# A hybrid decoder step on one core: cached pages copied later, unused products while x is loading, and gate blocks laid between products of 16 columns

## What is computed

```
u = rmsnorm(x)
z = u @ w_in + b_in                       # 1024 x 6968: mLSTM, queries, keys/values, gates
h_m = mlstm(conv(z[mx]), z[mv], z[mo], z[mi], z[mf], state_C, state_n, state_m)
h_n = nsa(z[nq], z[nkv], z[ng], cache_kv[page_table], cache_win_kv, w_cmp)
      # three branches: compressed blocks, selected blocks, a window
g   = sigmoid(z[bg])                      # 2 x 1024 merge gates
x   = x + (g_m * (h_m @ w_bm) + g_n * (h_n @ w_bn)) @ w_out
x   = x + moe(rmsnorm(x))                 # 32 experts, top 4
y   = rmsnorm(x)
```

## Time and profile before

| | us |
|---|---|
| median of 3 runs | 1617.41 (1616.68 to 1617.52) |
| profiled execution, its own time | 1614.81 |
| its span, first to last instruction | 1613.2 |
| TensorE busy | 1512.4 (94%) |
| VectorE / ScalarE / GpSimd busy | 545.6 / 317.4 / 53.1 |

### The profile page before, as it was taken

How to read it: one execution, slowest core, us unless ns; L and a number is a source line. 1 busy time by engine, 2 the same in 40 slices (tenths; PEclk the granted TensorE clock), 3 DMA queues, 4 the chain that set the end, 5 groups by cost and what they waited for, 6 DMA issues and landing times.

```text
span 1613.2 us, 22042 instructions
## 1 busy us (share of the span) xinstructions
PE 1512.4 (94%) x8565; PEld 710.6 (44%) x8565; DVE 545.6 (34%) x1184; ACT 317.4 (20%) x711; POOL 53.1 (3%) x121
## 2 busy tenths in 40 slices
PE   8999998999888899999999999999999999999996
PEld 5447555666755565433333333333333333333332
DVE  4511333444345422442323232232322222322323
ACT  2301221244235500311111111111111111111112
POOL 5410000000000000000000000000000000000000
PEclk9999999899999999999999999999999999999999
DMA  9932456152454299399999999999999999999995
GB/s 340 392 119 105 122 179 131 54 182 103 144 157 135 85 231 393 128 380 426 428 427 427 427 428 429 427 427 427 428 429 427 427 428 427 429 427 427 427 427 223
DMA packets 99712, 507.33 MB, mean 314 GB/s; under 512 B 19126, under 2 KB 57386, under 8 KB 73896
## 3 DMA queue, kind: packets, MB, share of 16 engines
q1 hardware_dynamic: 95522, 482.78, 75.4%
q0 software_dynamic: 4080, 23.73, 3.9%
q10 hardware_dynamic: 54, 0.05, 0.0%
HBM read 499.38 MB, written 28.06 MB: 327 GB/s over the span
## 4 chain that ended last, share of the span: by engine, by line
PE 31%; DMA 30%; DVE 3%; issue 1%; SPq 0%; ACT 0%; DVEq 0%
DMA wring<-w_gu 25%; PE bank L2116 14%; PE bank L2157 8%; DMA zf<-w_gu 4%; PE bank L1968 3%; PE bank L1977 2%; PE bank L2058 1%; PE bank L1953 1%; DMA wring<-w_branch_n 1%; DVE zf L2487 1%; DVE zf L2485 1%; DVE zf L2489 1%; PE bank L1986 0%; PE bank L1949 0%; PE bank L2091 0%
## 5 line engine op out<-in xcount | busy, mean ns | idle before, releaser
L2116 PE MATMUL bank<-wring,zf 128*64 128x512 f32 x1600 | 360.5, 596 | 25.2 <-DMA wring<-w_gu 24.8
L2116 PEld LDWEIGHTS bank<-wring,zf 128*64 128x64 f32 x1600 | 108.8, 136 | 250.5 <-issue 192.4
L2469 DVE SCALAR_TENSOR_TENSOR x<-bank,wt,x 128x512 f32<-128x512 f32 x155 | 104.9, 744 | 196.5 <-PE bank L2058 196.5
L2157 PE MATMUL bank<-wring,zf 128*64 128x512 f32 x768 | 170.1, 595 | 0.7
L2200 ACT ACTIVATE zf<-bank 128x512 f32<-128x512 f32 (+1 forms) x133 | 75.8, 594 | 314.5 <-PE bank L2157 214.8
L2116 PE MATMUL bank<-zf 128*64 128x512 f32 x448 | 100.8, 596 | 6.3 <-DMA zf<-w_gu 6.3
L2475 DVE TENSOR_TENSOR zf<-bank,zf 128x512 f32<-128x512 f32 x32 | 22.1, 692 | 224.6 <-ACT zf L2200 224.6
L2157 PEld LDWEIGHTS bank<-wring,zf 128*64 128x64 f32 x768 | 53.4, 137 | 98.9 <-issue 96.9
L954 PE MATMUL bank<-uT,w_slots 128*128 128x320 f32 x256 | 80.7, 463 | 1.2 <-ACT zf L1087 1.2
L1968 PE MATMUL bank<-zf,wring 128*128 128x320 f32 x256 | 69.4, 433 | 1.7 <-PEq L1279 0.9
L2058 PE MATMUL bank<-zf,eqw 64*128 64x512 bf16 x558 | 69.3, 380 | 0.0
(11 more groups left out here) (528 smaller groups left out, 1689.3 us busy)
## 6 DMA issues: line engine op xcount, KB each, us to landing
wring<-w_gu SPq DMA_DIRECT2D x100, 2048.0 KB, 32.6
wring<-w_dn SPq DMA_DIRECT2D x48, 2048.0 KB, 34.5
zf<-w_gu SPq DMA_DIRECT2D x28, 2048.0 KB, 32.8
zf<-w_dn SPq DMA_DIRECT2D x16, 2048.0 KB, 34.4
w_slots<-w_in SPq DMA_DIRECT2D x11, 2048.0 KB, 8.8
kv_linear<-cache_kv POOLq DMA_DIRECT2D x64, 256.0 KB, 5.2
kv_stage<-kv_linear SPq DMA_DIRECT2D x16, 1024.0 KB, 9.2
w_slots<-w_in SPq DMA_DIRECT2D x4, 1024.0 KB, 8.2
```

Source lines behind the costliest of these rows:

```text
L2116: last = pe.matmul(half(2 + gu, h), xe[:, k % 4, k // 4, :], m.ring[slot(k // 2)][:, o:o + H], start=False, stop=(k == KD - 1))
L2157: last = pe.matmul(half(4, h), atT[:, k % 4, k // 4, :], m.ring[slot(4 + k // 4)][:, o:o + H], start=(k == 0), stop=(k == 7))
L2469: dve.scalar_tensor_tensor(part(r), m.bank[SCATTER_BANKS[r]][:, :], wt[:, r // 2, bass.ds(i - 1, 1)], part(r), ALU.mult, ALU.add).then_inc ...
```

## The change

Three edits in `front` and three in `attend_prompt`:

- POOL waits for `s_pd` at 4 (four of the eight first blocks done) before the first page copy.
- TensorE issues 10 unused products as soon as DVE's chain gives its first signal, and 14 more after the mask products. They multiply a part of `qm` that DVE has set to zero, 128 x 128 x 128, and write bank 7, from which nobody reads them.
- `fill` is taken apart into `fill_product(n)`, n = 0 to 31 for blocks 0 to 3. Only halves 0 and 1 (block 0) stay ahead of the scores. Products 8 to 19 lie among the 16-column products, after steps 1, 4 and 7 of each eight. Then come half 5, the transpose and half 6, and products 28 to 31 lie among the 15-column products, one after each four pairs.
- ACT evicts block 0 first, block 1 after the exponentials of turns 0 and 1, and block 2 after the upper halves of the compression.

```diff
@@ front, POOL
             pool.wait_ge(s_pages, 16)
+            pool.wait_ge(s_pd, 4)
             for b in range(NB):
@@ front, TensorE
+            def stay_busy(n):
+                for _ in range(n):
+                    pe.matmul(m.bank[7][:, 0:128], qm[:, 0, 0:128], qm[:, 0, 0:128], start=True, stop=True)
+
+            pe.wait_ge(s_chain, 1)
+            stay_busy(10)
             pe.wait_ge(s_id, 2)
             pe.wait_ge(s_period, 7)
...
             pe.matmul(m.bank[3][:, 0:128], period[:], period[:], start=True, stop=True).then_inc(s_mk, 1)
+            stay_busy(14)
             pe.wait_ge(s_p, 160)
@@ attend_prompt, TensorE
-            def fill(half):
-
-                j, k0 = half // 2, 4 * (half % 2)
+            def fill_product(n):
+
+                j, k = n // KD, n % KD
                 chunk = C_BG + j // 4
-                if k0 == 0:
+                if k == 0:
                     if j % 4 == 0:
                         pe.wait_ge(m.s_win[chunk % NSL], chunk_count(chunk))
                     if j > 0:
                         pe.wait_ge(s_fe, j)
-                for k in range(k0, k0 + 4):
-                    last = pe.matmul(...)
-                if k0 > 0:
-                    last.then_inc(s_fd, 1)
+                out = pe.matmul(...)
+                if k == KD - 1:
+                    out.then_inc(s_fd, 1)
+
+            def fill(half):
+                for k in range(4):
+                    fill_product(4 * half + k)
...
-            for half in range(6):
+            for half in range(2):
                 fill(half)
...
                         last = pe.matmul(m.bank[4 + g][:, i * CST:(i + 1) * CST], m.wc[g * HD:(g + 1) * HD, i, r, :],
                                          m.kT[g * HD:(g + 1) * HD, i, r:r + CST * NC_P + 1:CST], start=(r == 0), stop=(r == CST - 1))
+                    if r % 8 in (1, 4, 7):
+                        fill_product(8 + i * 6 + r // 8 * 3 + r % 8 // 3)
             last.then_inc(s_c, 1)
-            fill(6)
+            fill(5)
             pe.wait_ge(s_ck, 1)
             pe.transpose(m.bank[5][0:NC_P, 0:128], cvT[:, :], m.ident[:, :]).then_inc(s_ct, 1)
-            fill(7)
+            fill(6)
...
+                    if u % 4 == 3:
+                        fill_product(28 + 2 * T + u // 4)
             last.then_inc(s_cs, 1)
@@ attend_prompt, ACT
-            for j in range(3):
-                evict_fill(j)
+            evict_fill(0)
             exps(0)
             exps(1)
+            evict_fill(1)
             act.wait_ge(s_c, 1)
...
             last.then_inc(s_ce, 1)
+            evict_fill(2)
             act.wait_ge(s_ct, 1)
```

More of the change, by code:

```diff
@@ L952, in fill @@
                         pe.wait_ge(s_fe, j)
-                for k in range(k0, k0 + 4):
-                    last = pe.matmul(m.bank[7][:, 0:NTOK], m.w_slots[:, chunk % NSL, k, j % 4 * 128:(j % 4 + 1) * 128],
-                                     m.uT[:, k, :], start=(k == 0), stop=(k == KD - 1))
-                if k0 > 0:
-                    last.then_inc(s_fd, 1)
+                out = pe.matmul(m.bank[7][:, 0:NTOK], m.w_slots[:, chunk % NSL, k, j % 4 * 128:(j % 4 + 1) * 128],
+                                m.uT[:, k, :], start=(k == 0), stop=(k == KD - 1))
+                if k == KD - 1:
[3 more added lines that the diff above has]
+                    fill_product(4 * half + k)
             def scores(U):
```

## The result

| | before | after |
|---|---|---|
| median of the runs | 1617.41 us | 1628.96 us |
| the profiled execution | 1614.81 us | 1628.96 us |
| its span | 1613.2 us | 1627.3 us |
| mean granted clock in it | 0.989 | 0.975 |

The ratio after to before is 1.0067, with a 95% interval of 1.0041 to 1.0093: slower by 0.7%. One of the five runs after took 3924.89 us, in a slow state, and is not in the ratio; the other four lie between 1623.38 and 1629.71. The forecast was 1602.8 us, in a range of 1598.5 to 1611, so the time lies 18 us above the range, on the other side of no change.

The account below looks back on a forecast made before the run. TensorE, busy nearly throughout the earlier stages, was taken as the bound. Front 6.8 + 3.3 + 1.8 = 11.9 us plus prompt 2.7 made 14.6: 1617.41 - 14.6 = 1602.8 us, range 1598.5 to 1611.

Parts of the forecast that it names:

- what bounds the kernel: Whole kernel: TensorE is busy nearly throughout the earlier stages, so a microsecond off its order there comes off the end.
- the copies: Front: page copies run from about 33.4 to 106 us, no chunk late; gain 3.3 us of wait and 1.8 of clock.
- price of 13.6 us: Front: time a chunk of w_in needs when alone with the page copies, taken for every chunk; over 4 us to spare.
- Rival 3: Front: later copies hold back chunks 2 to 5 by 24.9 us each; slower, 1626.9 us; chance 0.05.
- the unused products: Front: they raise the clock early, the first block ends at 20.5 us instead of about 27.3; gain 6.8 us (5.5 to 7.2).
- rival 2: Front: products on zeros, or spaced as these are, never raise the clock; 1617.6 us, no change; chance 0.08.
- rival 1: Front: the clock does not carry through the transposes of x, first block begins at about 21.5; 1609.3 us; chance 0.20.
- the 128 small records at the upper level cost ... 7.4 us; twelve products at 0.57 add 6.8: Prompt's attention: the 16-column products with gate products among them run at the upper clock, ending at 291.5 us.
- if the clock still falls once, some 3.5 us at the lower level cost 1.7 to 3.5 us: Prompt's attention: allowance for one clock fall, making the prompt's part 4 us gained to 1.5 lost.
- 16 changes, +3.2 to -1.0: Prompt's attention: changes between small and large products may expose or hide weight loads; bounds in us, taken as nothing.
- new wait for wc: Prompt's attention: transfers of wc keep the queues busy until 277.4 us, no longer hidden behind two blocks; 1.6 us.
- a clock of 0.50 among the mixed products: Prompt's attention: a sign named as showing the forecast wrong, the lower clock level where gate and small products are mixed.

Follow-up runs that it names:

- e3_copies_only: The kernel before with only the page copies moved behind four first blocks: 1611.28 us, ratio to before 0.9944.
- e4_unused_only: The kernel before with only the 24 unused products added in the front: 1615.47 us, ratio to before 0.9997.
- e9_threes_wait: The changed kernel with the twelve gate products in four groups of three, the wait for wc left: 1615.54 us, ratio to before 0.9998.
- e2_prompt_only: The kernel before with only the prompt's edits, the front as before: 1635.5 us, ratio to before 1.012.
- e1_front_only: The kernel before with only the front's edits (later copies, unused products), the prompt as before: 1607.01 us, ratio to before 0.9958.
- e5_dense_wait: The changed kernel with six more unused 320-column products on real data in place of the wait for wc: 1626.17 us, ratio to before 1.0065.
- e6_two_at_each: e5_dense_wait with two gate products at each of the twelve places, 24 in all, evictions earlier to match: 1615.26 us, ratio to before 0.9985.
- e10_24_singles: e6_two_at_each with the same 24 products and evictions, but no product beside another: 1620.87 us, ratio to before 1.0014.
- e11_runs: The changed kernel with blocks 0 and 1 ahead, then runs of 3, 3 and 2 products, half blocks later, evictions adjusted: 1608.26 us, ratio to before 0.9936.
- e7_groups_of_three: e5_dense_wait with the twelve gate products in four groups of three, one behind each 32 small records: 1614.19 us, ratio to before 0.9968.

## Why the prediction was wrong, step by step

**Right: what bounds the kernel.** What was gained and lost up to the transposes of probabilities came out at the end of the span almost in full (5.0 - 19.8 + 0.7 = -14.1).

**Right: the copies, with less to spare than forecast.** The forecast had them on POOL from 33.4 to 106; they began at 40.67 and were issued by 112. No chunk was late: the third landed 9.8 us after its issue where 24.9 had been needed. But the price of 13.6 us for a chunk beside the copies was too low: the fourth took 15.8, and the next two are (loads of `w_slots` issued from 60 to 100 us in after, shortest, median, longest)

```profile
DMA to landing us min/median/max: 11.8/14.6/17.5
```

The longest is inside the 18.3 that the forecast allowed by 0.8 us, not by over 4. The wait of 3.33 and the 1.8 us of clock are gone, and e3_copies_only shows the gain alone: 9.1 us by its ratio (5.3 to 12.8; 5.1 forecast). Its profile shows 5.9 us by the end of that block (75.36 against 81.29) and not where more would come from. Rival 3 is out, if narrowly: it decides from 18 us a chunk on.

**Right mechanism, wrong size: the unused products.** Zeros do raise the clock, so rival 2 is out. But the front gave less than the sum, for three reasons. First, the transposes of x cost 4.57 us for 24 at the upper level (13.12 to 17.69 in e4_unused_only), 0.19 each, not 0.113. The price came from a sample stage's transposes of 128 rows, while x's come in threes of 128, 128 and 64 rows. The nearer row was there before, in the same timeline as the earlier trace rows: 22 transposes of such a pattern at the upper level, 0.195 each.

```profile
256.71 4.28 PE L549 MATMUL bank<-ident,reused 64*128 64x64 f32 x22 [0.80 <-DVE reused L854]
```

That is 24 x 0.077 = 1.9 us. Second, the clock that was gained early did not stay: in after it is 0.50 from 9.1 to 12.5 and again from 15.9 to 22.7,

```profile
9.00:12.40 3.40, 3.40 (x19) 0.51 1.04 392
12.50:15.80 3.30, 3.30 (x30) 1.00 1.04 387
15.90:22.70 6.80, 6.80 (x21) 0.50 1.04 315
```

so the first block began at 20.40, not 16.2, and 2.3 us of it ran at the lower level. This is rival 1's mechanism in part, and only in some executions: of the ten profiles with the unused products the 24 transposes fell in two (6.34 us in after, 6.12 in e9_threes_wait) and ran through at the upper level in eight (4.64). The Trainium skill, "TensorE: Matmul & The Clock Gate", Part 4 (PE-mode transpose), says that transposes do not count as activity the way products do; the rows agree with it in after and not in e4_unused_only. Third, 1.7 us of the front's gain were given back ahead of the prompt's stage: the transposes of `reused` start 6.7 us earlier (250.01 against 256.71) and then take 5.96 us instead of 4.28, most of it at the lower level. That is no effect of the front: e2_prompt_only, whose front is that of before, has it too (6.00 us at 256.83), and e1_front_only does not (4.28). Forecast for the front 11.9 us; the profile of after gives 5.0, that of e1_front_only 8.6, and the ratio of its runs 6.8 (1617.41 x 0.0042). Of the two edits the runs credit the copies with it: with the copies late, leaving the unused products out changes nothing that can be measured (0.9941 against 0.9936, and 0.9944 against 0.9958).

**The step that failed: "the 128 small records at the upper level cost ... 7.4 us; twelve products at 0.57 add 6.8".** The 14.2 us were 28.4. The step took the upper level for granted and gave no reason for it. With one product among 8 to 12 small records they neither kept it up (e5_dense_wait, with no wait ahead) nor brought it back (30.7 us at 0.50 in after). And the hedge behind it, "if the clock still falls once, some 3.5 us at the lower level cost 1.7 to 3.5 us", took the length of a fall from before, where a dense half block stood behind the small products and the clock came back within it. The change took that half block's products apart and left the next dense run behind the whole mix. So the price of a fall was read from an order that the change removes. Two things made it dearer. The gate products, which used to run at 0.57 us, went to the lower level with the small records: the eleven in the stretch took 14.4 us (one at 0.74, ten at 1.37) for 6.3, and the small records the other 14.0 for 7.4. And at either level a single product among small ones costs 0.17 to 0.3 us more than in a row (0.74 for 0.57, and 1.37 for 2 x 0.54). The second was in the forecast's bounds (16 changes, +3.2 to -1.0) and taken as nothing; by e6_two_at_each and e10_24_singles it is 0.16 us for each change, into a product or out of it. The forecast counted one for each of the 16 products; with the way back there are some 30, about 4.8 us by this figure (an estimate), above the upper bound.

**Smaller terms of the prompt.** From the end of the stretch to the 15-column products it took 8.1 us (301.68 to 309.74) where 5.2 were forecast (2.3 + 0.62 + 2.3), since the first half block ran at the lower level: 2.9 us. The 15-column part up to its last product took 8.8 us (309.74 to 318.50) for 5.4, as the clock fell again at about 312.8: 3.4 us. What follows up to the transposes took 6.5 us (318.50 to 325.04) for 5.4: the last product, a wait of 0.71 and the half block ran at the lower level and were no longer hidden behind the chain through DVE, since no wait for it is left at 325.04: 1.1 us. The new wait for wc was forecast at 1.6 and came at 2.67 us; the stalls for evictions were forecast at 0.62 and came at 0.51 and 0.71. The forecast implied 47.3 - 2.7 = 44.6 us for the stage up to the transposes of probabilities, and 67.1 were measured; of the 22.5 us between them the stretch is 14.2, these three are 2.9, 3.4 and 1.1, and the later start of the stretch is 1.0 (15.3 us into the stage, where 277.3 - 262.95 = 14.35 were forecast).

**The rivals.** Each was drawn up for the front; the slower side was given to late chunks. The prompt's mix had a bound of 1.5 us lost, and no rival. So nothing in its chances priced what happened, and that rival 3's 1626.9 lies 2 us from the measured time is luck. The sign that it named as proof of error, "a clock of 0.50 among the mixed products", is what came; of its other signs, chunks in 14 us or less, transposes of x at about 0.12 us and mixed products with no 0.50 failed, and the token block at 13.9 without a wait held.

**What stays open.** Which property of the mix the clock answers to is not settled: groups of three hold it where as many singles do not, and twice as many singles do. The second fall of after in the front, and how late the unused products raise the clock (below), differ from execution to execution, and one profile for each kernel does not tell how often.

## What to carry to other kernels

Before spreading dense work among small products, ask what the clock stands on now: here a TensorE without a gap ran at 0.50 for 30.7 us, and before the clock came back only within the dense half block that stood behind the small products. Keep such filling work in runs of several products, put it where it also covers the wait ahead, look for where the clock falls next (in e11_runs that took the gain back), and take the price of a clock fall from the order that the change makes, not from the one that it removes. A transfer that nobody reads before 260 us should not run ahead of one that is needed at 62: here that one line was worth as much as the best version with all the edits.

## What the hardware showed unexpectedly

- The clock fell and stayed at 0.50 for 30.7 us while TensorE was busy without a gap (275.3 to 306 in after). With the same products three in a row it was back at 1.00 within 3.4 us of the same wait's fall (279.2 to 289 in e9_threes_wait).
- The same unused products, started at the same time, raised the clock at different times: at 4.6 us in the profile of e6_two_at_each, 5.65 in after, 7.0 in e4_unused_only, 14.6 in e7_groups_of_three.
- A change of tile shape costs time: 0.16 us each at 1.00 between records of 64x16 and of 128x320 (e6_two_at_each against e10_24_singles). And 24 transposes with one of 64 rows in every three take 0.19 us each at 1.00, where 52 of 128 rows take 0.113. The change of height is not all of that: the step from one 128-row transpose to the next is 0.17 us there too (13.69 to 13.86 in e4_unused_only). What the rest is stays open.
